# Product and diagonals of each pair of experts moved ahead of the side work of the same step

## Reference

```
act  = gelu(sum(u[idx] * x))          # one dot of 1024 per position and expert
coef = softmax(best_scores) * act
out  = sum(coef * v[idx])             # over 8 heads x 16 experts
```

## Time and profile before

| what | value |
|---|---|
| median of 3 runs | 1704.35 us (1704.04 to 1709.86) |
| the profiled execution | 1712.91 us, span 1711.1 us |
| PE busy | 1230.4 us (72% of the span) |
| DVE busy | 1195.4 us (70%) |
| ACT busy | 484.9 us (28%) |
| POOL busy | 602.0 us (35%) |
| moved by DMA | 670.19 MB, mean 392 GB/s |
| gathers of experts | 512, 540.65 MB with the rest of their queue |
| weights | 60 chunks, 127.65 MB with the rest of their queue |
| chain that ended last | DMA 34%, PE 30%, DVE 22%, issue 7%, ACT 4% |
| GB/s in 40 slices | 302 197 302 423 382 423 418 422 422 395 424 421 315 424 421 408 395 325 425 422 422 422 305 420 421 422 411 341 381 423 422 420 421 421 422 421 421 422 421 242 |

### The profile page before, as it was taken

One profiled execution on the slowest core, in us unless ns is written; L12 is line 12 of the kernel. 1 busy time (PEld: TensorE's weight loads), 2 busy tenths in 40 slices (PEclk: granted clock), 3 DMA queues, 4 the chain that ended last, 5 costly groups with the idle time before them and its releaser, 6 DMA issues.

```text
span 1711.1 us, 21732 instructions
## 1 busy us (share of the span) xinstructions
PE 1230.4 (72%) x7384; PEld 593.8 (35%) x7384; DVE 1195.4 (70%) x3389; ACT 484.9 (28%) x1123; POOL 602.0 (35%) x525
## 2 busy tenths in 40 slices
PE   6865886757849978968695699696869656645554
PEld 2453232215516744422361376342226311111111
DVE  3356678766586888885755688889665787777755
ACT  0122124212213544621232244363112222222211
POOL 1023424433332322334233233331433444455451
PEclk9987888888967989979896699897989866787786
DMA  8579999999998999989999799998999999999995
GB/s 302 197 302 423 382 423 418 422 422 395 424 421 315 424 421 408 395 325 425 422 422 422 305 420 421 422 411 341 381 423 422 420 421 421 422 421 421 422 421 242
DMA packets 84076, 670.19 MB, mean 392 GB/s; under 512 B 9376, under 2 KB 9520, under 8 KB 10624
## 3 DMA queue, kind: packets, MB, share of 16 engines
q0 software_dynamic: 74608, 540.65, 76.8%
q1 hardware_dynamic: 9216, 127.65, 17.9%
q10 hardware_dynamic: 144, 0.52, 0.1%
HBM read 667.74 MB, written 1.05 MB: 391 GB/s over the span
## 4 chain that ended last, share of the span: by engine, by line
DMA 34%; PE 30%; DVE 22%; issue 7%; ACT 4%; POOL 2%; ACTq 0%; DVEq 0%; POOLq 0%; SPq 0%; PEldq 0%
DMA ring<-in_experts,idx 32%; PE acc L737 13%; PE act_bank L485 10%; DVE ring L1272 7%; PE dve_bank L471 3%; DVE scratch L931 3%; DMA wbuf<-in_weights 2%; POOL ring L428 2%; DVE h L1293 1%; DVE onehot L931 1%; PE act_bank L718 1%; ACT scratch L772 1%; ACT diag L898 1%; PE act_bank L471 1%; ACT L772 1%
## 5 line engine op out<-in xcount | busy, mean ns | idle before, releaser
L428 POOL DMA_INDIRECT ring<-in_experts,idx x512 | 596.0, 1164 | 1061.8 <-PE acc L737 853.0
L737 PE MATMUL acc<-ring,diag 64*64 64x512 f32 x4096 | 642.3, 757 | 332.8 <-ACT diag L898 318.7
L1272 DVE CUSTOM_DVE_ANT_0 ring<-ring,hn 128x1024 f32<-128x1024 f32 x512 | 622.7, 1224 | 265.0 <-DMA ring<-in_experts,idx 247.1
L737 PEld LDWEIGHTS acc<-ring,diag 64*64 64x64 f32 x4096 | 160.2, 160 | 721.6 <-ACT diag L898 466.2
L891 ACT ACTIVATE acts<-dots 128x2 f32<-128x2 f32 x256 | 52.0, 203 | 775.1 <-DVE dots L1272 752.0
L485 PE MATMUL act_bank<-hnT,wbuf 128*128 128x128 f32 x2048 | 255.7, 283 | 15.6 <-ACT hnT L772 10.9
L485 PEld LDWEIGHTS act_bank<-hnT,wbuf 128*128 128x128 f32 x2048 | 242.5, 197 | 60.0 <-issue 57.6
L898 ACT ACTIVATE diag<-cst,coefs 128x64 f32<-128x64 f32 x512 | 150.3, 340 | 204.8 <-DVE coefs L1280 173.5
L1280 DVE TENSOR_TENSOR coefs<-acts,gate 128x2 f32<-128x2 f32 x256 | 41.4, 162 | 96.9 <-ACT acts L891 86.3
L772 ACT ACT_TABLE_LOAD x77 | 98.8, 1283 | 11.7 <-DMA rowc<-in_rows 9.6
L471 PE MATMUL dve_bank<-wbuf,scratch 128*128 128x512 f32 x192 | 94.5, 628 | 1.0 <-ACT scratch L772 0.7
(11 more groups left out here) (125 smaller groups left out, 834.0 us busy)
## 6 DMA issues: line engine op xcount, KB each, us to landing
wbuf<-in_weights SPq DMA_DIRECT2D x60, 2048.0 KB
ring<-in_experts,idx POOLq DMA_INDIRECT x512
scratch<-in_bias POOLq DMA_DIRECT2D x1, 1024.0 KB, 11.3
out<-h SPq DMA_DIRECT2D x2, 512.0 KB
scratch<-in_bands POOLq DMA_DIRECT2D x1, 768.0 KB, 6.5
h<-in_x SPq DMA_DIRECT2D x1, 512.0 KB, 3.9
gains<-in_gains POOLq DMA_DIRECT2D x1, 512.0 KB, 4.9
h<-in_x POOLq DMA_DIRECT2D x1, 512.0 KB, 18.1
```

Of the source, the lines that this page charges most:

```text
L428: pool.indirect_dma_start(ring[:, n % RING], None, io[f"experts{layer}"], bass.IndirectOffsetOnAxis(idx[:, at:at + 1], 0),).then_inc(sem(f ...
L737: last[rows] = pe.matmul(acc[rows][half][home:home + HALF_P], diag[part, n % DIAGS], ring[part, slot, D + half * CW:D + (half + 1) * CW], ...
L1272: dve.tensor_tensor_reduce(out=ring[:, slot, 0:D], in0=ring[:, slot, 0:D], in1=hn[:, phase % NBLK], scale=1.0, scalar=0.0, op0=ALU.mult, o ...
```

## The change

In the odd step of every pair, VectorE multiplies gelu and gate directly behind the second dot, ahead of the mixer's and the routing's share. ScalarE makes the pair's diagonals directly behind its gelu, ahead of both shares. Nothing is added or taken out.

```diff
@@ ScalarE, experts @@
                     if n % GROUP == GROUP - 1:
                         take_gelu(g, q)
+                        make_diagonals(g, q)
                     beside.upto(pace(phase, n))
                     routes.upto(routes_due(phase, n))
-                    if n % GROUP == GROUP - 1:
-                        make_diagonals(g, q)
@@ VectorE, experts @@
                     g = first + n // BODY
                     dot(phase, g, n % BODY)
+                    if n % GROUP == GROUP - 1:
+                        coefficients(phase, g, n % BODY // GROUP)
                     if n == GROUP and phase:
                         add_experts(phase - 1)
...
                     if n >= GROUP or not phase:
                         beside.upto(pace(phase, n))
                     routes.upto(routes_due(phase, n))
-                    if n % GROUP == GROUP - 1:
-                        coefficients(phase, g, n % BODY // GROUP)
```

## The result

The changed kernel takes 1724.28 us (median of 4 runs, 1722.59 to 1732.39), beside 1705.51 us for the kernel before on the same chip (median of 4, three of them the runs of the table ahead of the prediction): ratio 1.0115, 95% interval 1.0078 to 1.0152, some 19 us slower. The forecast was 8 us slower, 1712.5 us, with a range of 1698 to 1728 us. The time lies in that range and the sign was right, but the loss is over twice the forecast one; its size is that of the larger-loss rival, 1723 us. The profiled execution took 1724.26 us, its span is 1722.4 us. Lines of the experts' code are one lower than before (dot 1271, product 1279).

A forecast was written before the change was run, and what follows sets the result against it. Transfers bound the kernel, with VectorE's order moving the end only beside the two scans; net costs of 4.5 and 3.6 us there, together 8 us, on the 1704.35 us median gave 1712.5 us, range 1698 to 1728 us.

The forecast's parts named there:

- larger-loss rival: Convolution stages: late gelus and bare round trips add 11 us on top of 8, 1723 us; chance 0.18.
- What bounds the kernel: Whole kernel: held by transfers at some 422 GB/s; VectorE's order moves the end only at 633 to 750 and 1077 to 1192.
- the starvations: Stretches with idle DMA engines at 740 to 760 and 1180 to 1200 us, losing 8.6 and 9.9 us of their 20.
- the faster rival: Two scan stretches: earlier diagonals let TensorE sum earlier and free slots earlier, 11 us faster, 1693 us; chance 0.17.
- Products bare beside the scans: Beside the two scans: 14 and 13 products show the bare 0.27 us round trip, 3.8 and 3.5 us.
- late gelus: Beside the two scans: gelus start late while ScalarE is still in the even step's side work, 2.3 and 0.8 us.
- Diagonals ahead of exps: Odd steps beside the scans: product and diagonals delay the decays' exp at four and three places, 2.2 and 1.8 us.
- what is given back: Beside the two scans: VectorE waits less for ScalarE, TensorE and a gather, 3.8 and 2.5 us taken off the cost.
- Everywhere else at nothing: Outside the two scan stretches, convolutions included: no cost, since DMA engines are full with 25 us of queue ahead.
- the 318.7 us: Whole kernel: TensorE's wait for the diagonals, which looks like the fault that the change is aimed at.
- Hidden: Whole kernel: the DMA queue or ScalarE's and TensorE's slack takes up all, 0 to 3 us, 1706 us; chance 0.15.
- lose DMA share: Convolution stages: a lost DMA share there would show the forecast wrong; no size given.

The follow-up runs named there:

- rest: Kernel before, with the new order only in phases 0 and 3 and in steps 66 to 127 of phases 1 and 2: 1704.51 us, +0.8 us.
- only_scan: Kernel before, with the new order only in steps 32 to 65 of phases 1 and 2, beside the scans: 1715.75 us, +10.5 us.
- coefs_only: Kernel before, with products directly behind the dots in all phases and diagonals at their old place behind ScalarE's shares: 1716.56 us, +11.3 us.
- only_conv: Kernel before, with the new order only in steps 0 to 31 of phases 1 and 2, phase starts and convolutions: 1718.21 us, +14.5 us.
- all_but_scan: Kernel before, with the new order everywhere but in steps 32 to 65 of phases 1 and 2: 1716.8 us, +11.6 us.
- two_pairs: Kernel before, with the new order only in steps 19 and 23 of phases 1 and 2, four pairs of 256: 1709.08 us, +3.8 us.
- between: Kernel before, with product and diagonals everywhere behind the mixer's share and ahead of the routing's share: 1706.93 us, +3.3 us.

## Why the prediction was right in sign and short in size

**What bounds the kernel.** Held. The 190 pairs of `rest`, with DMA engines full and little mixer work, take the edit at 0.8 us. Three readings were off without weight. VectorE does not work without a gap from 633 to 750 us: the waits shown in the earlier trace rows add up to 11.6 us. The 3.6 us called a wait for TensorE have no releaser in that row; the second trace names TensorE's sequencer, 3.0 us. And the losses in the starvations were taken from the DMA share; by GB/s they are 4.6, 9.1, 1.2 and 10.4 us, 25 in place of 21.5, which moves the faster rival to 1692 us.

**Products bare beside the scans.** Held, and sized a little low. `only_scan` measures 10.5 us for the forecast's 8; its interval, 6 to 14 us, holds it. Dot by dot, against the kernel before run again, steps 32 to 67 of phases 1 and 2 took 7.1 and 5.4 us longer in `only_scan`. VectorE's idle time in them, added over the timelines: 9.3 and 6.7 us for gelu, where it was 0.5 and 0.9. That is 8.8 and 5.8 us more, and the terms for bare and late gelus were 3.8 + 2.3 and 3.5 + 0.8, so 14.6 us came where 10.4 stood. The late gelus are the mis-sized ones, that of step 33 above all, 1.9 and 2.3 us in `only_scan`. Beside them stands a term that I had not seen, 1.1 us in each: where a dot follows VectorE's own side work and no longer the product, it starts 0.2 us later.

**Diagonals ahead of exps, and what is given back.** Both show in VectorE's wait for ScalarE's side work. It fell from 7.8 to 5.0 us and from 2.4 to 0.2 us in the same steps. I had it above 6.8 us between 633 and 750; there it is 5.0. `coefs_only`, with the diagonals at their old place, takes the two apart: there the wait is 2.6 and 0.2 us. So the diagonals ahead of exps cost 2.4 us in the first scan, as the 2.2 had it, and nothing of this kind in the second, where 1.8 stood (three places at 0.55 us are 1.65). And what is given back, 5.2 and 2.2 us for 3.8 + 2.5, comes from the early product: it is there without the early diagonals. By the dots the early diagonals cost 1.6 us in each scan, at the limit of what single traces tell, and more in the convolutions, where they stand ahead of PSUM evictions; the whole is 18.8 less 11.3, 7.5 us.

**Everywhere else at nothing.** This is the step that failed, for its convolution part. The queue of 25 us was read at one gather, at 607 us, near its deepest, and taken as cover for all that the stage could lose; 40 us later it was 11 us in the same kernel. `only_conv` measures 14.5 us. Part of the stage's waits is swallowed indeed: in steps 8 to 31 of phases 1 and 2 the changed kernel's VectorE waits 9.6 and 9.8 us more for gelu, but 3.6 and 3.3 us less for gathers and 2.2 and 4.9 us less for ScalarE's side work. The rest, 4.2 and 1.6 us by the dots with 2 us of uncertainty on each, goes through, and the queue ran dry at 650 us.

**The larger loss.** Its mechanism holds: it put the added waits at 22 us in the convolution steps, half of them real, +11; the trace has 21.8 us more, and `all_but_scan` has +11.6, `only_conv` +14.5. That its sum, 1723 us, meets 1724.28 is in part luck: the scans cost more than its 8, the parts do not add up, and its count of three gelus of about 3 us in each stage met two of 4.65 to 4.85 and 3.34 us. It fell in the reason for taking half. I had written that the lateness of gelus is itself made by late diagonals and would shrink. It did not. In step 19 the product waited 3.35 us in `two_pairs`, 4.0 and 2.7 in `coefs_only`, where the diagonals stay late, and 4.65 and 4.85 in the changed kernel, where early diagonals delay evictions and these delay TensorE. Its condition, that VectorE's lag passes to TensorE, was met at the scan's first product. It was met the other way round as well: TensorE's lag came back to VectorE. It had a chance of 0.18 and deserved the larger one; DVE busy for 79.77 of 93 us and PE for 82.98 left 13 and 10 us of slack in a stage with 16 products to be laid bare and several late gelus.

**Faster and hidden.** Earlier diagonals brought nothing in any kernel. The Trainium skill's advice (Perfetto Trace Analysis, Optimization Strategy), to make what ends the gaps of the engine in question start sooner, picks the 318.7 us when it is applied to TensorE, the engine with the largest busy share. The runs show that row to be slack: 13 us less of it with 19 us more of time here, and in `rest` 303.5 us with no change of time. Hidden, 0 to 3 us, is what `rest` shows for its 190 pairs; for the whole kernel the interval, 1.0078 to 1.0152, excludes it.

**Signs.** Right: products' waits 144.3 us (120 to 150 forecast), 420 to 424 GB/s in full stretches, the starvations later (the emptiest 5 us, from 745 and from 1185 us in the second trace of the kernel before, begin at 755 and 1205; some 4 us later was forecast). Slightly off: ScalarE's wait for products 57.9 us (60 to 80). Misleading: the convolution stages were to lose DMA share if I was wrong; from 540 to 633 they kept all of it, and the loss showed first at 650.

**What stays open.** How the changed kernel's 19 us divide between bare round trips, TensorE's lower clock and its later projections in the convolution steps: each was seen, none was taken away by itself. So it is argued, not shown, that the later eviction at step 15 makes the long wait of step 19 longer. And why `between` is slightly above the kernel before, beyond the 3 us of gelu waits in its scans.

## What to carry to other kernels

On engines that work in order, a short operation with a round trip through another engine belongs behind the work that hides the trip. Before moving it forward, count how often its wait is zero today (103 of 256 here): each such place will show the bare trip, here 0.27 us, and everything behind it pays. A large wait at the consumer (318.7 us) is worth nothing while transfers are full; but a full queue covers only a lag shorter than itself, so look for where it is next close to empty, in the stage behind, and for side work through which the lag can reach the instruction that frees a buffer. And what is put ahead of a PSUM eviction delays TensorE, which can then cost twice: the delay, and the lower clock behind it.

## What the runs showed of the hardware

- The same 32 matmuls of 128x128 took 3.81 us behind idle times of 0.79 to 1.55 us (13 times) and 5.26 to 5.44 us behind 1.80 to 3.93 us (15 times), with the granted clock at 0.52 from 564 to 566 us in the changed kernel. From 1.36 to 2.94 us of idle time, 1.6 us more of waiting cost 1.5 us more of work.
- The bare trip from the end of a dot through gelu to the product is 0.27 us where ScalarE is free; two more gelus of 0.20 us each raised the products' waits by 114 us over 256 pairs (258.3 less 144.3), 0.45 us each.
